# Neighbourhood attention on one Trainium2 core: scores, turns and values of two units at a time

## The reference

```python
def row_step(r):
    qr = lax.dynamic_index_in_dim(qg, r, axis=2, keepdims=False)
    kr = lax.dynamic_slice_in_dim(kg, rs, wr, axis=2)[:, :, :, col_idx]
    vr = lax.dynamic_slice_in_dim(vg, rs, wr, axis=2)[:, :, :, col_idx]
    ...
    logits = jnp.einsum('bhcd,bhicjd->bhcij', qr, kr).astype(jnp.float32) * scale + bias[None]
    p = jax.nn.softmax(logits.reshape(b, h, GRID_W, wr * NA_WIN_C), axis=-1)
    return jnp.einsum('bhcij,bhicjd->bhcd', p, vr)
...
    y = jnp.concatenate([out_a * jax.nn.silu(g_a), out_b * jax.nn.silu(g_b)], axis=-1)
    x = x + y @ w_out[l]
```

## Time and profile before

| what | value |
|---|---|
| time, median of 3 runs (lowest to highest) | 935.06 us (934.2 to 935.72) |
| span of the profiled execution | 933.6 us |
| mean granted TensorE clock | 0.998 |
| TensorE busy | 898.7 us, 96% of the span |
| VectorE busy | 577.9 us, 62% |
| ScalarE busy | 450.8 us, 48% |
| GpSimd busy | 111.1 us, 12% |
| the stage in the first layer (score of unit 3 to `out_rows(1)`) | 560.66 to 590.91 us |
| the same in the second layer | from 855.04 us |

### The profile page before, as it was taken

The page is one execution under the profiler, slowest core; times in us unless marked ns, Lnnn a source line. Parts: engine busy times, 40 slices in busy tenths (PEclk is TensorE's granted clock), DMA queues, the critical chain, the costliest instruction groups (busy, mean ns, idle before and its releaser), DMA issues.

```text
span 933.6 us, 14669 instructions
## 1 busy us (share of the span) xinstructions
PE 898.7 (96%) x5733; PEld 707.6 (76%) x5733; DVE 577.9 (62%) x1170; ACT 450.8 (48%) x964; POOL 111.1 (12%) x137
## 2 busy tenths in 40 slices
PE   3999999999999999999999999999999999999996
PEld 1679888774667788887788886788887778887785
DVE  5899798988887472438953447245255975435633
ACT  4634324566785243426925349233334863435731
POOL 1001120005100010000010007200000010003702
PEclk9999999999999999999999999999999999999999
DMA  9735646266000332323204334122243222334103
GB/s 378 318 96 135 184 141 181 102 181 238 34 2 4 111 130 91 113 90 88 94 18 139 107 94 133 43 91 91 91 142 98 72 91 91 91 91 136 46 23 91
DMA packets 34678, 104.69 MB, mean 112 GB/s; under 512 B 14961, under 2 KB 14961, under 8 KB 32178
## 3 DMA queue, kind: packets, MB, share of 16 engines
q1 hardware_dynamic: 28098, 85.77, 27.6%
q0 software_dynamic: 3856, 15.73, 5.4%
q10 hardware_dynamic: 2656, 2.26, 1.0%
HBM read 98.37 MB, written 4.19 MB: 110 GB/s over the span
## 4 chain that ended last, share of the span: by engine, by line
PE 90%; DVE 4%; ACT 3%; issue 1%; DMA 1%; SPq 0%; POOL 0%; POOLq 0%; DVEq 0%; ACTq 0%
PE bank L1059 82%; PE bank L1419 2%; PE bank L1399 2%; PE bank L1558 1%; DMA ring<-in_w_ada 1%; PE bank L1475 1%; DVE arena L1686 0%; ACT ring L977 0%; PE bank L1465 0%; ACT ring L868 0%; ACT w_hi L916 0%; ACT arena L749 0%; ACT soft L984 0%; DVE xn_t L2197 0%; DVE w_lo L2172 0%
## 5 line engine op out<-in xcount | busy, mean ns | idle before, releaser
L2172 DVE TENSOR_TENSOR w_lo<-ring,w_hi 128x1024 fp32r<-128x1024 f32 x80 | 97.8, 1225 | 114.6 <-ACT w_hi L916 111.5
L1059 PE MATMUL bank<-w_hi,hT_hi 128*128 128x512 f32 x320 | 125.6, 393 | 1.3 <-issue 1.0
L1059 PE MATMUL bank<-hT_hi,w_hi 128*128 128x512 f32 x320 | 126.3, 395 | 0.0
L1059 PE MATMUL bank<-w_lo,hT_hi 128*128 128x512 f32 x320 | 124.7, 390 | 0.0
L1059 PE MATMUL bank<-hT_lo,w_hi 128*128 128x512 f32 x320 | 124.6, 389 | 0.0
L1059 PE MATMUL bank<-hT_hi,w_lo 128*128 128x512 f32 x320 | 124.6, 389 | 0.0
L1059 PE MATMUL bank<-w_hi,hT_lo 128*128 128x512 f32 x320 | 124.5, 389 | 0.0
L916 ACT ACTIVATE w_hi<-ring 128x1024 fp32r<-128x1024 f32 x80 | 84.4, 1058 | 11.6 <-PE bank L1059 11.4
L1059 PEld LDWEIGHTS bank<-w_hi,hT_hi 128*128 128x128 f32 x320 | 60.1, 188 | 15.0 <-issue 2.9
L1059 PEld LDWEIGHTS bank<-hT_hi,w_hi 128*128 128x128 f32 x320 | 60.1, 188 | 14.0 <-issue 0.7
L1059 PEld LDWEIGHTS bank<-hT_lo,w_hi 128*128 128x128 f32 x320 | 60.1, 188 | 12.7
(11 more groups left out here) (324 smaller groups left out, 1803.8 us busy)
## 6 DMA issues: line engine op xcount, KB each, us to landing
ring<-in_w_units SPq DMA_DIRECT2D x80, 512.0 KB, 3.7
ring<-in_w_ada SPq DMA_DIRECT2D x4, 2048.0 KB, 10.2
bias_ring<-in_na_bias POOLq DMA_DIRECT2D x6, 1024.0 KB, 5.3
ring<-in_w_out SPq DMA_DIRECT2D x2, 2048.0 KB, 8.5
bias_ring<-in_t_bias POOLq DMA_DIRECT2D x8, 448.0 KB, 3.7
x_t<-in_x SPq DMA_DIRECT2D x4, 512.0 KB, 6.1
arena<-in_w_ada SPq DMA_DIRECT2D x1, 2048.0 KB, 20.3
arena<-in_w_ada SPq DMA_DIRECT2D x2, 1024.0 KB, 23.2
```

Source lines behind the costliest of these rows:

```text
L1059: return pe.matmul(out, lhsT, rhs, start=first, stop=last)
L2172: dve.tensor_tensor(w_lo[:, u % 4], raw_w[:, u % 4], w_hi[:, u % 4].bitcast(fp32), SUB).then_inc(S["w_split"], 1)
```

## The change

TensorE's loop of the stage steps by two units. It issues the scores of two units, then the turns of two, then the weighs of two. ScalarE's loop still goes unit by unit, but issues the exponentials of unit j ahead of the move of unit j - 3, where it was the move first. The first part of the first output tile (`out_rows(0)`) is issued at j = 17, after the turns of units 14 and 15 and the weighs of 12 and 13.

```diff
                         for j in range(N_EARLY, N_NA + NA_LAG):
-                            na_move(l, j - NA_LAG)
                             if j < N_NA:
                                 na_exp(l, j)
+                            na_move(l, j - NA_LAG)
...
-                        for j in range(N_EARLY, N_NA + NA_LAG + 1):
-                            if j < N_NA:
-                                na_score(l, j)
-                            if j <= N_EARLY + 1:
-                                pe.wait_ge(S["proj_evac"], pt2(l, 8) - 1 + j - N_EARLY)
-                            if j < N_NA + NA_LAG:
-                                na_turn(l, j - NA_LAG)
+                        for j in range(N_EARLY, N_NA + NA_LAG + 2, 2):
+                            for m in range(j, min(j + 2, N_NA)):
+                                na_score(l, m)
+                            if j == N_EARLY:
+                                pe.wait_ge(S["proj_evac"], pt2(l, 8))
+                            for m in range(j - NA_LAG, min(j - NA_LAG + 2, N_NA)):
+                                na_turn(l, m)
                             if j > N_EARLY:
+                                na_weigh(l, j - NA_LAG - 2)
                                 na_weigh(l, j - NA_LAG - 1)
-                            if j == N_NA:
+                            if j == N_NA + 1:
                                 out_rows(0, 6, range(0, 4))
```

## The result

| | before | changed |
|---|---|---|
| time, median (lowest to highest) | 935.1 us (934.2 to 935.72), 4 runs | 940.49 us (939.24 to 941.34), 4 runs |
| ratio, 95% interval | | 1.0054 (1.0042 to 1.0066) |
| span and mean granted clock, the four runs | | 937.4 at 0.998, 938.0 at 0.997, 939.3 at 0.995, 939.5 at 0.994 |
| stage, first layer (score of unit 3 to `out_rows(1)`) | 30.25 us | 32.55 us |
| stage, second layer | 30.25 us | 33.64 us |

The change made the kernel slower by 5.4 us. The forecast was 938.8 with 940.4 as its upper end. The profiled execution is the one of 941.34 us. The four runs lie in the order of their clock: the less clock was granted, the longer the span. That was not in the prediction.

The account below looks back on a forecast made before the run. TensorE and ScalarE were taken as full at once, so batching gains nothing; the uncovered wait for GpSimd's last scale adds 2.24 + 1.46 = 3.7 us over the two layers, giving 938.8 us, range 937.5 to 940.4.

Parts of the forecast that it names:

- ScalarE full, the batches' saving a wait: Steady part: batches save 0.49 us a pair, but second turns wait for ScalarE's move, so a pair still takes 3.45.
- the walk: Instruction-by-instruction calculation over four engine queues with paces and latencies from the rows; it gave 3.7 us slower in all.
- Turns and weighs back to back: On TensorE, a turn or weigh behind one of its kind costs 0.44 us, against 0.59 as now.
- The second rival: TensorE's turns and weighs gain nothing from batching, 0.59 us each: 5.0 us slower, 940.1 us; chance 0.12.
- The end of the stage: Turn of unit 15, ahead of `out_rows(0)`, waits 1.8 us for GpSimd's scale; first layer's `out_rows(1)` 2.24 us later.
- The third rival: End of stage: GpSimd reaches the last scale early, so only 1.4 us slower, 936.5 us; chance 0.09.
- The second layer: No transfer issued there, so scale at 585.76 and turn at 586.85 on the first layer's clock; `out_rows(1)` 1.46 us later.
- 1.4 us around the span: Time outside the profiled span, added to the forecast span of 937.3 us to give 938.8 us.
- The fourth rival: TensorE's bubbles set the pace and ScalarE follows: up to 6.4 us faster, 928.7 us; chance 0.05.

Follow-up runs that it names:

- the kernel with fillers: The changed kernel plus matmuls whose results nobody reads in TensorE's gaps, at the stage's start and ahead of the turn of unit 15: 938.87 us, ratio 1.0039.
- The cover given back: The changed kernel with the first output rows put back ahead of the turns of units 14 and 15: 936.11 us, ratio 1.0014.
- The last pair of experiments: First high part moved ahead of unit 3's exponentials: on TensorE's pairs with ScalarE's old order and output rows ahead of turns 14/15, 934.66 us; on the kernel before, 934.74.
- TensorE's pairs alone: The kernel before with TensorE's pairs and output rows behind the turn of unit 15, ScalarE's order of before: 941.08 us, ratio 1.0066.

## Why the prediction held, and where it was short

**ScalarE full, the batches' saving a wait.** Right. TensorE's busy time in the steady part fell by 1.15 us, and ScalarE's stayed 13.80 of 13.80. First turns of pairs stand 3.43 to 3.48 us apart, the second turns waited 0.26 to 0.33 us for the move, at 570.73, 574.23, 577.63 and 581.09 where the walk had 570.49, 573.94, 577.39 and 580.84; the constant 0.25 is what came ahead of the stage.

**Turns and weighs back to back.** Right for turns, a little short for weighs. I took 0.44 for both, four steps of 0.11, under the bound of 0.59. Weighs stand 0.49 apart. For turns the wait hides it in most pairs, but the eight matmuls of two turns span 1.09 us where nothing stands between them (562.34 in the kernel with fillers), against 0.66 for four: 0.43 more. The second rival needed 0.59 for both. The rule of the Trainium skill behind it ("TensorE: Matmul & The Clock Gate", "Part 3: Packing small matmuls — row/col tiling") is not what these rows show.

**The end of the stage.** Right in mechanism and size: 2.30 us measured for the first layer, 2.24 forecast; the turn of unit 15 at 587.90 against 587.63, its wait 1.62 in the rows and 1.8 in the walk. Four terms were off and nearly cancel there: the transfer's issue took 0.60 against 0.78, while the scale of unit 14 came 0.08 later, the turn followed its scale after 1.20 in place of 1.09, and `out_rows(1)` the turn after 5.56 in place of 5.44. The cover given back removes 4.4 us in the median, and 5.5 with ScalarE's order of before, so the wait is also the cause. The third rival, a short tail, would need GpSimd to reach the last scale early; it was made so by hand, and then the one run at full clock took 936.05.

**The second layer.** This is the term that was mis-sized: "`out_rows(1)` 1.46 later", where 3.39 was measured. The walk gave every matmul one pace. It counted TensorE's waits at the start of the stage (for VectorE's take and for the first moves) as free because ScalarE set the end. In that execution half clock followed them for 6.83 us, the scores and turns under it came late, GpSimd then idled 1.94 us ahead of a scale at 868.99, and its own queue was late from there on. By the estimate from the kernel with fillers 1.68 of the 3.39 us are there at full clock, 0.2 more than forecast: this layer has no issue there, so nothing cancels the terms that were too short. The other 1.7 us go with the clock. For the whole the runs without falls say 939.24 (the changed kernel at 0.998, one run) and 938.87 (fillers), the forecast 938.8. Its range up to 940.4 had no place for the clock, and the median of 940.49 lies 0.1 above it. So the mechanism at full clock was right, and the 1.7 us by which the median lies above the forecast are mostly a price that the sum had left out. The sum was also made with 1.4 us around the span by the median of before; where a run has both a time and a span they are about 1.8 apart, which would make the sum 939.1; the 1.4 came of setting one span against a median of other runs.

**The fourth rival, faster.** It asked for the exponentials of unit 15 at 581.5; they came at 583.95, at the same distance from the score of unit 3 as before. The last pair of experiments bears out the reason: with the same 0.52 us off ScalarE the stages with pairs shrink by 0.5 us and are 0.37 and 0.08 us shorter than those without.

What stays open: why the second layer of TensorE's pairs alone takes 0.7 us more than the walk at full clock, of which 0.2 is accounted for; why the same gaps go with a lower clock in one execution and not in the next; and which engine holds the pairs once ScalarE has more room.

## What to carry to other kernels

Batching one engine's work saves nothing where a second engine is full over the same stretch; read both engines' busy time by windows before counting the saving. Work that covers a wait for a slower engine (here an output tile ahead of the last turns) is worth more than the order of the instructions around it: moving it cost 4.4 of 5.4 us. And idle time on TensorE had a price beyond its own length here, where a stretch at half clock followed it; an edit that turns TensorE's work into waits should be measured in many runs, with the granted clock beside each time.

## What the runs showed of the hardware beyond this

The granted clock fell to 0.50, that is 1.2 of 2.4 GHz, for 3.41 or 6.83 us at a time, in the changed stage of six of the twelve profiled executions. Ahead of it TensorE had stood idle once or several times, for 0.5 to 2.6 us a time: busy 3.06 of 5.63 us, 3.26 of 5.51, 3.92 of 5.68 and 3.33 of 5.09 in the stretches ahead of it that are shown here. The Trainium skill tells of this gate in "TensorE: Matmul & The Clock Gate", section "HAM oscillation — how this bites in real kernels", for waits on transfers; here the waits ahead of the falls are for VectorE, ScalarE and GpSimd, none longer than 2.57 us, and the same waits stand in executions and layers without a fall. With matmuls that serve for nothing in such gaps the profiled execution kept its clock in both stages, and the median was 1.6 us lower. And a low part of 0.67 us on VectorE took up to 2.00 beside a scale on GpSimd.
